# Moving the second scale's column sums in front of the last output projection job, and the first MLP weight split behind the last residuals

## What is computed

```python
mod = c @ w_ada + b_ada                       # 6 x 2048 columns
sh1, sc1, gt1, sh2, sc2, gt2 = split(mod, 6)
...
y = concatenate([ya, yr]) @ w_out             # output projection
x = x + gt1 * y
h2 = rmsnorm(x, g_ffn) * (1 + sc2) + sh2
f = square(relu(h2 @ w1)) @ w2                # MLP, 2048 -> 8192 -> 2048
x = x + gt2 * f
return rmsnorm(x, g_final)
```

## Time and profile before

| what | value |
|---|---|
| median of 3 runs | 1176.98 us (1175.03 to 1178.56) |
| span of the profiled execution | 1176.1 us |
| TensorE busy | 1132.5 us, 96% |
| VectorE busy | 795.4 us, 68% |
| ScalarE busy | 492.5 us, 42% |
| mean granted TensorE clock | 0.992 |

### The profile page before, as it was taken

How to read it: one execution, slowest core, us unless ns; L and a number is a source line. 1 busy time by engine, 2 the same in 40 slices (tenths; PEclk the granted TensorE clock), 3 DMA queues, 4 the chain that set the end, 5 groups by cost and what they waited for, 6 DMA issues and landing times.

```text
span 1176.1 us, 15924 instructions
## 1 busy us (share of the span) xinstructions
PE 1132.5 (96%) x6339; PEld 957.8 (81%) x6339; DVE 795.4 (68%) x690; ACT 492.5 (42%) x517; POOL 21.1 (2%) x27
## 2 busy tenths in 40 slices
PE   3879999999999999999999999999999999999996
PEld 1769989788778878888888888888888888888885
DVE  2577889987878898866565566565566565565675
ACT  2424454555534445443333444333444333444451
POOL 2000010000000001000000000000000000000000
PEclk9999999999999998999999999999999999999999
DMA  9999989999997956766666676666676666665551
GB/s 351 368 348 397 381 319 339 338 403 390 357 404 269 322 182 223 252 222 229 235 230 185 188 222 228 235 228 186 187 220 229 238 224 187 187 196 180 180 177 72
DMA packets 156749, 303.10 MB, mean 258 GB/s; under 512 B 5425, under 2 KB 73633, under 8 KB 148129
## 3 DMA queue, kind: packets, MB, share of 16 engines
q1 hardware_dynamic: 155248, 298.08, 72.4%
q10 hardware_dynamic: 832, 2.93, 0.6%
q0 software_dynamic: 624, 1.48, 0.4%
HBM read 300.36 MB, written 2.10 MB: 257 GB/s over the span
## 4 chain that ended last, share of the span: by engine, by line
PE 91%; DVE 4%; DMA 3%; issue 1%; ACT 1%; ACTq 0%; SPq 0%; DVEq 0%
PE ps_job L924 20%; PE ps_job L963 14%; PE ps_job L964 14%; PE ps_job L965 14%; PE ps_job L927 10%; PE ps_job L939 3%; PE ps_job L940 3%; PE ps_job L941 3%; DMA stage<-in_w_ada 2%; PE ps L1030 1%; DVE acc L1247 1%; DVE w_lo L1323 1%; DMA cst<-in_consts 1%; PE ps_job L1211 1%; PE ps_job L1209 1%
## 5 line engine op out<-in xcount | busy, mean ns | idle before, releaser
L1323 DVE TENSOR_TENSOR w_lo<-stage,w_hi 128x2048 fp32r<-128x2048 f32 x164 | 375.8, 2292 | 218.5 <-ACT w_hi L518 218.3
L518 ACT ACTIVATE w_hi<-stage 128x2048 fp32r<-128x2048 f32 (+1 forms) x167 | 318.0, 1904 | 424.0 <-PE ps_job L965 231.4
L924 PE MATMUL ps_job<-act_hl,w_hi 128*128 128x512 f32 x1024 | 322.4, 396 | 1.5 <-DVE w_lo L1323 1.1
L927 PEld LDWEIGHTS ps_job<-act_hl,w_lo 128*128 128x128 f32 x1024 | 192.7, 188 | 45.0
L927 PE MATMUL ps_job<-act_hl,w_lo 128*128 128x256 f32 x1024 | 201.2, 278 | 0.0
L963 PE MATMUL ps_job<-w_hi,hid_hl 128*128 128x512 f32 x480 | 188.1, 392 | 0.0
L964 PE MATMUL ps_job<-w_lo,hid_hl 128*128 128x512 f32 x480 | 187.0, 390 | 0.0
L965 PE MATMUL ps_job<-w_hi,hid_hl 128*128 128x512 f32 x480 | 186.9, 389 | 0.0
L924 PEld LDWEIGHTS ps_job<-act_hl,w_hi 128*128 128x128 f32 x1024 | 156.1, 189 | 2.5 <-DVE w_lo L1323 1.3
L1247 DVE SCALAR_TENSOR_TENSOR acc<-stage,small,acc 128x2048 f32<-128x2048 f32 (+1 forms) x56 | 122.9, 2195 | 7.2 <-DMA stage<-in_w_ada 3.5
L963 PEld LDWEIGHTS ps_job<-w_hi,hid_hl 128*128 128x128 f32 x480 | 90.1, 188 | 19.2 <-issue 0.7
(11 more groups left out here) (223 smaller groups left out, 1127.1 us busy)
## 6 DMA issues: line engine op xcount, KB each, us to landing
stage<-in_w SPq DMA_DIRECT2D x128, 1024.0 KB, 5.3
stage<-in_w_ada SPq DMA_DIRECT2D x64, 1024.0 KB, 7.8
stage<-in_w_in SPq DMA_DIRECT2D x41, 1024.0 KB, 8.5
stage<-in_w_ada SPq DMA_DIRECT2D x32, 512.0 KB, 6.9
stage<-in_w_out SPq DMA_DIRECT2D x16, 1024.0 KB, 7.7
gate_rows<-in_w_ada SPq DMA_DIRECT2D x16, 1024.0 KB, 7.0
x_sb<-in_x ACTq DMA_DIRECT2D x1, 2048.0 KB, 13.5
out_y<-f_acc SPq DMA_DIRECT2D x3, 512.0 KB, 2.7
```

What stands on the lines that cost most here:

```text
L518: nc.scalar.activation(w_hi[:, ring, 0:width], stage[:, slot, 0:width], ACT.Copy).then_inc(hi_ready, 1)
L924: nc.tensor.matmul(ps_job[:, 2 * pair + e, :], w_hi[:, ring, ws], act_hl[:, kt, :], start=(kt == 0), stop=False)
L927: last = nc.tensor.matmul(ps_job[:, 2 * pair + e, T:2 * T], w_lo[:, ring, ws], act_hl[:, kt, 0:T], start=False, stop=(kt == KT - 1))
L1323: nc.vector.tensor_tensor(w_lo[:, ring, 0:width], stage[:, slot, 0:width], w_hi[:, ring, 0:width].bitcast(F32), ALU.subtract).then_inc(lo_ ...
```

## The change

Three edits. `turn_rows` moves from behind the last output projection job into the first group of job `J_MLP-2` (`G_MLP-4`), between its second and third slice of four. `sum_mod(0, 3)`, with its wait for the last scaled row, moves behind the last gate spread, so in front of the last job's 48 products. On VectorE the shift and scale copies move in front of `mean_so_far`, and the split of `G_MLP` from in front of it to behind the last residuals.

```diff
@@ token_group
                         if in_halves is not None and (k, t) == (2, 0):
+                            if in_halves == G_MLP - 4:
+                                turn_rows()
                             pe.wait_ge(lo_ready, READY[ITEM_OF_GROUP[in_halves]])
@@ TensorE, behind each group of the output projection
                     spread_gate(n, n % 2)
+                    if n == STRIPS - 1:
+                        pe.wait_ge(lo_ready, READY[ITEM_OF_TILE[5 * KT - 1]])
+                        sum_mod(0, 3)
 
             PB = J_MLP % 2
 
-            turn_rows()
-            pe.wait_ge(lo_ready, READY[ITEM_OF_TILE[5 * KT - 1]])
-            sum_mod(0, 3)
             for r in range(4):
@@ VectorE, behind the last group of the output projection
-            split_group(G_MLP, 0, 0, G_MLP + 1)
+            dve.wait_ge(mod_summed, 5)
+            nc.vector.tensor_copy(shift2, ps[:, 2, 0:KT]).then_inc(mod_ready, 1)
+            nc.vector.scalar_tensor_tensor(out=scale2, in0=ps[:, 3, 0:KT], scalar=1.0, in1=vec_T[:, V_FFN:V_FFN + KT],
+                                           op0=ALU.add, op1=ALU.mult).then_inc(mod_ready, 1)
             mean_so_far(2 * STRIPS)
             take_out(J_MLP - 1)
-
+            split_group(G_MLP, 0, 0, G_MLP + 1)
@@ VectorE, between the first and the second quarter
             normalise_quarter(0)
-            dve.wait_ge(mod_summed, 5)
-            nc.vector.tensor_copy(shift2, ps[:, 2, 0:KT]).then_inc(mod_ready, 1)
-            nc.vector.scalar_tensor_tensor(out=scale2, in0=ps[:, 3, 0:KT], scalar=1.0, in1=vec_T[:, V_FFN:V_FFN + KT],
-                                           op0=ALU.add, op1=ALU.mult).then_inc(mod_ready, 1)
             normalise_quarter(1)
```

## The result

The changed kernel takes 1182.02 us (median of 13 runs, 1179.46 to 1184.23) against 1176.99 us (13 runs, 1175.03 to 1181.32). The ratio is 1.0038, with a 95% interval of 1.0026 to 1.0049: slower by 4.5 us (3.1 to 5.8); the medians differ by 5.0 us. The forecast was +4.5 us and 1181.5 us.

What follows compares the result with a forecast made beforehand. TensorE, busy 96% of the span and full through the MLP, was taken as the bound. Terms 3.5 + 1.5 - 0.5 = +4.5 us took the span from 1176.1 to 1180.6, median forecast 1181.5 us, range 1179.0 to 1185.2.

Steps and rivals of the forecast that it cites:

- +3.5 us for the passes: In front of the last job on TensorE, 32 column-sum passes with nothing hiding them: +3.5 us (3.2 to 6.4).
- +1.5 us for the clock: Low granted clock on the rest of the sums or the last job's products: +1.5 us (0 to about 3.3).
- about 3.3: Upper end of the clock term: two low-clock stretches in a row around the last job, about 3.3 us.
- -0.5 us for the tail: From the last job's end to ScalarE's first modulation, 6.55 us instead of 7.02: -0.5 us (0 to -1.6).
- The lower end of -1.6: Best case of the tail term behind the last job, if the moved split cost nothing: -1.6 us.
- the row turn: In job J_MLP-2's first group, 0.79 us covered by a 1.18 us hole: cost 0, or 0.8 without cover.
- the copies: VectorE's two shift and scale copies, 0.17 us each, wait for nothing when moved; no gain beyond the tail's 0.5.
- ScalarE's rounding of the fifth group: Group five's load issues later behind the split, but ScalarE needs it with 20 us of room: cost 0.
- The clock that holds in front of the job: Rival: the clock does not fall on the sums before the last job; +3.0 us, 1180.0 us, chance 0.20.
- The clock that comes back later in the tail: Rival: after TensorE's idle time, first MLP products run at 0.50, losing 1.3 us: 1182.8 us or worse, chance 0.22.
- The sums in a wait: Rival: a late weight split makes TensorE wait before the last job, hiding the sums: 1176.5 us, chance 0.08.

Runs made afterwards that it cites:

- e1: Kernel before with only the split of the first MLP group moved behind the last residuals; 1177.17 us, ratio 1.0005.
- e4: Changed kernel with only 1 of the 16 column sums, so the output is not the layer's; 1178.24 us, ratio 1.0012 to the kernel before.
- e6: Changed kernel with the 16 column sums spread between products of the last job's first half; 1180.95 us, ratio 1.0031 to the kernel before.
- a1: The changed kernel run again unaltered, for a second look at the clock; 1182.60 us.
- e2: Changed kernel with the split of the first MLP group put back in front of the mean; 1180.95 us, ratio 1.0037 to the kernel before.
- e3: Kernel before with only the row turn moved into the first group of job J_MLP-2; 1176.05 us, ratio 0.9990.
- a2: The changed kernel run a third time unaltered; 1182.39 us.
- e10: Changed kernel with 1 of 16 column sums, plus 22 never-read dense products in TensorE's idle time behind the last job; 1176.45 us, ratio 0.9998 to the kernel before.

## Why the prediction was right

**The place was read right.** What is put between the spread and the last product was paid in full, and behind the job little came back. Both stand in the table: with the sums in a block in front the distance from spread to last product grows by 5.1 to 6.8 us, without them it is back at 11.6 to 11.8 (e1, e4), and the tail gives back 0.3.

**+3.5 us for the passes**: 3.69 in e6 (15.25 less 11.56), the cleanest measure, with the clock at 1.00 throughout.

**+1.5 us for the clock**: right for one stretch (1.45 in a1, 1.47 in e2), but two of the three profiles of the change have two stretches and pay 3.1, the end that I gave as about 3.3. The forecast's value is thus the smaller of two common cases, not the middle. The four profiles with the sums in a block in front of the job all lose the clock while TensorE is busy without a gap (in the change 1.50 of 1.50 us from 433.0 and 1.00 of 1.00 from 435.5), and the one with the same products spread between dense ones does not. The Trainium skill ("TensorE: Matmul & The Clock Gate", section "HAM oscillation — how this bites in real kernels") warns of idle gaps alone; that warning doesn't cover what happened here.

**-0.5 us for the tail**: -0.34 and -0.33 in two profiles of the change, 0 in a1. The quarter came when it was worked out (0.40 us after its old distance, from 4.53 to 4.93), and the transposes 5.87 us behind the last product's start, for which 5.9 (5.5 from its end) was forecast. What was off is the step from there to the modulation. The forecast took 1.06 us for it, from 451.06, where the sums end on the chain; but the transposes had started at 450.93, and from their start it is 1.19 us before and 1.21 us after (456.80 less 455.59). The lower end of -1.6 doesn't follow from the two figures in its bracket (5.4 less 4.1 is 1.3); 451.06 less 445.10 against 450.12 less 445.80 gives 1.6. Nothing else rests on it. The gain itself hangs on the clock: in e1, with the sums behind the job but hardly slowed, the modulation comes 7.09 us behind the last product, as in the change without them (7.08).

**The rest**: the row turn is free to 0.05 us (from spread to spread 13.10 us before, 13.11 with the change, 13.15 in e3); the copies wait for nothing in their new place, and ScalarE's rounding of the fifth group waits for TensorE for 2.59 us (at 478.61) as before, not for its load.

**The rivals.** The clock that holds in front of the job happened in none of the four profiles with the sums in a block. The clock that comes back later in the tail did happen (a1, e1, e4), but at 0.35 us in a1, not 1.3: of the 1.01 us that TensorE lost on the first rounds, 0.66 were taken up in front of the second group, where TensorE waits for VectorE in the change. In the changed kernel transposes were all that TensorE did between 450.1 and the clock's return just before 459.0. The Trainium skill ("TensorE: Matmul & The Clock Gate", section "Part 4: PE-mode transpose") states that the full clock doesn't engage for transposes; this profile doesn't bear that out. In a1, e1 and e4 the clock came back only after the first MLP products had begun; what decides between the two is not shown. The sums in a wait did not happen; the hole in front of the group before was filled by the row turn.

**What is luck.** In the profiled pair the path grows by 6.42 us (35.79 less 29.37): 3.69 for the passes, 3.07 for the clock, 0.34 back in the tail (a split of the one difference by e6, not a check on it). The three profiles of the change are 5.2 to 6.5 us over the one profile of the kernel before, and the ratio of the runs says 4.5 (3.1 to 5.8). That it meets the forecast's +4.5 to the tenth is in part luck, since two of the three profiles pay twice the clock term that was forecast. Why the runs show less than the paths is not shown: the last spread, which lies ahead of all this, came earlier in the three profiles of the change (431.19 to 432.72) than in the one of the kernel before (433.15), and one profile can't say whether 433.15 is usual.

## What to carry to other kernels

Before moving work off the end of a stage, look at what ends second there: here the column sums ended 0.9 us after the next contender, so at most that could be won by taking them away, and even that margin hung on the clock (in e1, where the quarter came 0.4 us later and the clock held longer, they were done 1.13 us before it), while in front of the job, where TensorE never waits, all of their passes are paid. Many products of one column are cheap to write and dear to place: they can also cost the clock of the dense products behind them, which mixing them with the dense ones avoided in e6. A wait already in the trace (the 1.18 us in front of one group) was the right place for small work of 0.8 us.

## What the runs showed that was not expected

Around the change the low clock lasted 3.4 us or twice that (6.8 us) wherever it came, and the same program got the one or the other on its last job (a1 against a2). And idle time of TensorE was not free where transposes and short rounds followed: dense products that nobody reads, put into it, brought the 16 transposes from 3.67 to 1.97 us (e4, e10) and the path 0.93 us down, though the times of the runs are too close to show it.
